# Last attention of a two-block transformer: the rotation of the next head's positional queries issued behind the third transposition instead of before it

## What is computed

```python
def queries(q_a):                       # q_a: 512 x 256
    q = (_rmsnorm(q_a, qa_norm) @ w_qb).reshape(B, L, MLA_HEADS, 128 + 64)
    return q[..., :128], q[..., 128:]

def _attend(q_nope, q_pe, k_nope, k_pe, v):
    s = (jnp.einsum('bqhd,bkhd->bhqk', q_nope, k_nope)
         + jnp.einsum('bqhr,bkr->bhqk', q_pe, k_pe))
    p = jax.nn.softmax(s * MLA_SCALE, axis=-1)
    return jnp.einsum('bhqk,bkhd->bqhd', p, v)

q_pe = _apply_rope(q_pe, cos, sin)      # x * cos + rotated(x) * sin
y_lat = (o.reshape(B, L, D_INNER) * jax.nn.silu(z)) @ w_out   # z: the gate
```

## Time and profile before

| what | value |
|---|---|
| median of 3 runs | 3926.66 us (3925.34 to 3934.91) |
| the profiled execution | 3928.54 us, its span 3926.7 us |
| granted TensorE clock, mean over the span | 0.948 |
| TensorE matmul busy | 3606.9 us, 92% |
| VectorE busy | 1635.3 us, 42% |
| ScalarE busy | 1077.5 us, 27% |
| steps of the head loop with a next head | 15, from about 3325 to 3765.53 us of the span |

### The profile page before, as it was taken

One profiled execution on the slowest core, in us unless ns is written; L12 is line 12 of the kernel. 1 busy time (PEld: TensorE's weight loads), 2 busy tenths in 40 slices (PEclk: granted clock), 3 DMA queues, 4 the chain that ended last, 5 costly groups with the idle time before them and its releaser, 6 DMA issues.

```text
span 3926.7 us, 51666 instructions
## 1 busy us (share of the span) xinstructions
PE 3606.9 (92%) x20408; PEld 2674.9 (68%) x20408; DVE 1635.3 (42%) x2657; ACT 1077.5 (27%) x1664; POOL 533.6 (14%) x252
## 2 busy tenths in 40 slices
PE   6888999999988889999989999999996987999988
PEld 4666578886556655775478888888885554666653
DVE  4455220000025652000048787787876033555521
ACT  3333111110013341111043343433431022444420
POOL 2220034440013203661000000000000000000000
PEclk8988999999999999999989999999997977999989
DMA  6222223332211013444211111111102111111111
GB/s 236 75 69 96 74 103 114 105 128 107 64 54 42 24 59 125 171 171 150 91 54 48 52 48 52 52 44 44 44 28 91 48 32 38 38 32 37 37 32 64
DMA packets 81447, 292.01 MB, mean 74 GB/s; under 512 B 8224, under 2 KB 10272, under 8 KB 80416
## 3 DMA queue, kind: packets, MB, share of 16 engines
q1 hardware_dynamic: 75632, 274.30, 20.8%
q10 hardware_dynamic: 5680, 15.73, 1.0%
HBM read 275.32 MB, written 14.68 MB: 74 GB/s over the span
## 4 chain that ended last, share of the span: by engine, by line
PE 87%; DVE 6%; ACT 3%; issue 1%; DVEq 1%; DMA 1%; ACTq 0%; SPq 0%
PE ps L474 38%; PE ps L459 23%; PE ps L969 5%; PE ps L835 2%; PE ps L529 2%; PE ps L704 2%; PE ps L1049 1%; PE ps L897 1%; PE ps L505 1%; PE ps L1032 1%; PE ps L908 1%; PE ps L787 1%; ACT arena L1325 1%; PE ps L538 1%; PE ps L764 1%
## 5 line engine op out<-in xcount | busy, mean ns | idle before, releaser
L474 PE MATMUL ps<-x_r,ringA_r 128*128 128x512 f32 (+1 forms) x2704 | 953.1, 352 | 24.3 <-ACT arena L1390 13.1
L474 PE MATMUL ps<-x_r,ringB_r 128*128 128x512 f32 (+1 forms) x2704 | 939.2, 347 | 13.2 <-DVE a_r L1621 13.1
L459 PE MATMUL ps<-arena,ringA 128*128 128x512 f32 (+1 forms) x2208 | 796.4, 523 | 13.9 <-DVEq L1669 8.6
L459 PEld LDWEIGHTS ps<-arena,ringA 128*128 128x128 f32 x2208 | 421.0, 191 | 388.8 <-issue 369.6
L474 PEld LDWEIGHTS ps<-x_r,ringA_r 128*128 128x128 f32 x2704 | 511.8, 189 | 109.7 <-issue 32.7
L474 PEld LDWEIGHTS ps<-x_r,ringB_r 128*128 128x128 f32 x2704 | 511.5, 189 | 93.6 <-issue 24.1
L474 PE MATMUL ps<-a_r,ringA_r 128*128 128x512 f32 x1600 | 542.3, 339 | 0.0
L474 PE MATMUL ps<-a_r,ringB_r 128*128 128x512 f32 x1104 | 394.9, 358 | 0.0
L423 POOL TENSOR_TENSOR ringB_r<-ringA,consts 128x1024 fp32r<-128x1024 f32 x104 | 197.2, 1896 | 981.9 <-DMA ringA<-streamA 981.9
L474 PEld LDWEIGHTS ps<-a_r,ringA_r 128*128 128x128 f32 x1600 | 303.1, 189 | 34.7 <-issue 1.0
L1698 DVE TENSOR_TENSOR arena<-arena,ps 128x768 f32 (+1 forms) x44 | 36.1, 821 | 623.5 <-ACT arena L1235 342.1
(11 more groups left out here) (269 smaller groups left out, 4661.7 us busy)
## 6 DMA issues: line engine op xcount, KB each, us to landing
ringA<-streamA SPq DMA_DIRECT2D x236, 512.0 KB, 3.7
arena<-streamC SPq DMA_DIRECT2D x136, 512.0 KB, 6.6
ringB<-streamB SPq DMA_DIRECT2D x100, 512.0 KB, 3.6
x<-x_in SPq DMA_DIRECT2D x2, 3072.0 KB, 11.7
x_scratch<-x ACTq DMA_DIRECT2D x6, 1024.0 KB, 5.2
a<-streamC SPq DMA_DIRECT2D x8, 512.0 KB, 11.8
x<-x_scratch SPq DMA_DIRECT2D x2, 2048.0 KB, 8.5
x_scratch<-x ACTq DMA_DIRECT2D x2, 1536.0 KB, 6.3
```

Source lines behind the costliest of these rows:

```text
L459: mm = nc.tensor.matmul(ps[0:m, bank + half, 0:tn], ring[:, slot, w0 + k * P:w0 + k * P + m], src[:, k0 + k, t0:t0 + tn], start=start and ...
L474: mm = nc.tensor.matmul(ps[:, bank + half, 0:tn], wk, src[:, k, t], start=k == 0 and i == 0, stop=k == DC - 1 and i == 2)
```

## The change

In TensorE's list the gate's sixth and seventh slices (numbers 5 and 6) both stand between `turn(1)` and `turn(2)`; the rotation and the eighth slice stand behind `turn(2)`. In VectorE's list `rope_q` stands behind `low(2)` instead of before it, and `positional_low` behind `low(3)`. In ScalarE's list `rotated` stands behind `copy_p(3)`. No instruction is added or removed.

```diff
                     turn(1)
                     if follow:
-                        gate(n, 1 - e, 5, 6)
+                        gate(n, 1 - e, 5, 7)
+                    turn(2)
+                    if follow:
                         rotate(n, 1 - e)
-                    turn(2)
-                    if follow:
-                        gate(n, 1 - e, 6, 8)
+                        gate(n, 1 - e, 7, 8)
                     turn(3)
...
                     copy_p(1)
                     copy_p(2)
+                    copy_p(3)
                     if follow:
                         rotated(n, 1 - e)
-                    copy_p(3)
-                    if follow:
                         gate(n, 1 - e)
...
                     low(1)
+                    low(2)
                     if follow:
                         rope_q(n, 1 - e)
-                    low(2)
+                    low(3)
                     if follow:
                         positional_low(n, 1 - e)
-                    low(3)
```

More of the change, by code:

```diff
@@ L1064, in step @@
                     if follow:
-                        gate(n, 1 - e, 5, 6)
-                        rotate(n, 1 - e)
+                        gate(n, 1 - e, 5, 7)
                     turn(2)
                     if follow:
-                        gate(n, 1 - e, 6, 8)
+                        rotate(n, 1 - e)
+                        gate(n, 1 - e, 7, 8)
                     turn(3)
```

## The result

The changed kernel takes 3946.63 us in the median of 5 runs (3945.01 to 3951.21), the kernel before 3931.54 us in the median of 5. The ratio is 1.0045, with a 95% interval of 1.003 to 1.006: 0.45% or 15.1 us slower. Forecast were 3942.3 us (3932 to 3952) and +15.6 us.

The account below looks back on a forecast made before the run. TensorE, busy 92%, bounds the kernel, each step's length set by when the output product starts. 12 steps at 30.7 us and 3 at 30.1, mean 1.04 over 29.54, times 15 give +15.6 us: 3942.3 us, range 3932 to 3952.

Parts of the forecast that it names:

- Part 1: TensorE around turn(2): gate slice forward, rotation behind; turn(2) stays tied to low(1), idle merges to about 2.3 us, gain nothing.
- Rival C: At turn(2): held by the rotation, not low(1), so it starts earlier; product 0.6 us earlier, -20 us, 3907; chance 0.04.
- Part 2: VectorE's rope_q behind low(2): the attention's output product starts at 3462.94 instead of 3461.67, +1.27 us a step at full clock.
- Rival D: Before the product: rope_q is ready before turn(3) ends, so no effect; 3927 to 3931 us; chance 0.05.
- Part 3: Same path at half clock: about +1.0 us, step of 30.9, or about +0.4, step of 30.5, by where the clock falls.
- The count of falls: TensorE's clock in the head loop: 12 of 15 steps with a fall at 30.7 us, 3 at full clock at 30.1.
- The total: All 15 changed steps: mean 30.58 us, 1.04 over 29.54, together +15.6 us, median 3942.3.
- Rival A: TensorE's clock falls in almost no step, recovering its losses: +8.0 us, 3934.7; chance 0.13.
- Rival B: New 1.2 us idle before the product brings a second clock fall during it: steps of 31.8, +34 us, 3961; chance 0.09.
- The rule that the prediction takes from the Trainium skill: Short idle stretches between matmul groups make TensorE's clock swing; taken strictly, each step falls: the upper end, 3947.

Follow-up runs that it names:

- The slice alone: Against the kernel before, only the gate slice moved ahead of the rotation and turn(2), VectorE and ScalarE keeping their order: 3920.54 us against 3929.63, ratio 0.9969.
- the filled loops: Unread matmuls in TensorE's idle stretches: changed kernel 3935.98 us (both stretches) or 3934.75 (first only), kernel before 3918.47; ratios to before 1.0016, 1.0015, 0.9971.
- VectorE's order alone: Against the kernel before, only VectorE's and ScalarE's new order taken over, TensorE keeping its list of before: 3944.82 us, ratio 1.0031.
- the one with the rotation back: Changed kernel with the rotation again before turn(2), behind the two slices, VectorE and ScalarE in the new order: 3945.53 us, ratio 1.0041 to the kernel before.

## Why the prediction was right

**Part 1, right.** turn(2) stayed where it was, at 17.54 us, tied to low(1) by 0.15 us. Rival C is out. The idle before it became one stretch of 2.30 us, the rotation lost its wait, and nothing waited for the moved one. The slice alone at full clock is worth nothing in the step.

**Part 2, right to the hundredth:** +1.27 us forecast, +1.27 in the step at full clock, 1.26 in the filled loops. Each of its terms stands in the rows of after: rope_q 0.88 us behind low(2)'s start, 1.36 to its last operation. The forecast for the step at full clock was 30.1 (30.0 to 30.1 measured). Rival D is out.

**Part 3, wrong in size.** The prediction had the clock return before turn(3), as in rows 7 and 8, and priced a step with a fall at 30.9 or 30.5. Five of them took 31.9 to 32.0, since the clock stayed down through the rotation, the slice and turn(3): 2.07 us for the slice instead of 1.12, 1.48 for turn(3) instead of 0.84. The product then starts at 24.05 us and no longer waits for rope_q. The term that failed is the assumption that a fall lasts as long as those seen before, whatever work follows it. With TensorE's list of before it did (+0.89 us in the run with VectorE's order alone, for about 1.0 forecast), with the changed list it didn't.

**The count of falls, wrong the other way.** 12 of 15 steps were forecast with a fall; 8 of 14 had one, against 9 before. Too many falls, each too cheap: 1.04 us a step forecast, 1.25 measured in the loop. The forecast had the falls cost 30.58 - 30.07 = 0.51 us a step in the changed kernel; they cost 10.17 / 14 = 0.73, as much as in before (0.74). That is why the measured step grows by nearly the full-clock difference.

**The total, in part by luck.** At 1.25 us a step 15 steps make 18.7 us, 3.1 more than the 15.6 forecast. The last step, which the forecast took as unchanged, gives 1.9 us back by its clock, so the loop as a whole is 16.8 us longer. The totals were 15.1 us over before in one comparison and 19.6 in the other, and the changed kernel's lowest and highest run lie 6 us apart in the first and 12 in the second. That 15.1 stands so near 15.6 is no proof of the sum. Nor is the nearness of the medians, 3946.63 to 3942.3: the forecast counted from 3926.66, three runs' median of before, which is 3931.54 in five.

**Rival A** had the clock recover all its losses. It didn't in this order, though three other orders show that it can. **Rival B** occurs, but with the rotation before turn(2), not in the changed kernel. The rule that the prediction takes from the Trainium skill ("TensorE: Matmul & The Clock Gate", section "A second HAM failure mode: psum-queue depth-cycling"), read strictly as a fall in each step, isn't what the changed kernel does; VectorE's order alone does just that.

What stays open is why the same sum of idle time falls in one step and not in the next. The runs show that it is the same in two executions and that it goes when the stretches are filled, and with the slice alone, which spreads them; but with VectorE's new order added the spread stretches had 9 falls again. The runs don't give a rule for it, nor for the clock in the last step.

## What to carry to other kernels

Before an operation is moved behind another on an engine, ask what ran beside it in its old place: rope_q was free because VectorE would have idled there, and cost 1.27 us a step where it went. When a wait on TensorE goes because its instruction moved, look whether the instruction behind it was waiting for the same engine anyway; then the idle time only gets longer in one piece. And where an engine's queue sets the pace, try splitting a group of operations: the part with slack can go back, the part that fills a gap should stay. A fall of the clock costs only what it moves on the path: behind a wait that ends later anyway it costs next to nothing.

## What the runs showed of the hardware

- TensorE's clock fell from 2.4 to 1.2 GHz behind idle stretches of 1.44 and 0.60 us in 9 of 14 steps, and in none where the same idle time stood as 0.64, 0.60 and 1.13 us. That alone was worth 10.3 us in the loop, 0.3% of the kernel, with the work unchanged. It isn't safe in general: with a further 1.03 us behind these three it fell in 9 of 14 steps again, in 4 of them already behind the 0.60.
- In the changed kernel and the one with the rotation back, a fall cost by its place: 0.2 us at most where the product waited for VectorE anyway, 0.3 where only the slice, turn(3) and the product's start were slow, 1.5 where it began with the product, 1.9 where it took in turn(2), the rotation, the slice and turn(3).
- Unread matmuls in the idle time (1.5 us of busy time a step) gave the same 10.4 us, the clock staying at 1.00.
- With VectorE's new order alone all 14 steps fell alike, at 30.68 to 30.77 us each; in the changed kernel the steps came in a fixed sequence of three kinds, the same in two traces.
- A multiplication of 128 x 512 numbers took 1.61 us on GpSimd and 0.68 us on VectorE.
